# Seven products instead of eight for the third matrix of three feed-forwards, and second-matrix units spread between later pairs

## The reference

```python
# block 1, layers 0 and 1: feed-forwards 1 and 2
f = (jax.nn.silu(h @ ffn_w1[l]) * (h @ ffn_w3[l])) @ ffn_w2[l]
x = x + g2 * f
...
# block 2, layers 0 and 1: feed-forwards 3 and 4
gate, up = jnp.split(x @ w_ffn_in[i], 2, axis=-1)
ffn = (jax.nn.silu(gate) * up) @ w_ffn_out[i]
x = layer_norm(ALPHA * x + ffn + ple, ln2_g[i], ln2_b[i])
```

## Time and the profile before

| | us |
|---|---|
| median of 3 runs | 2541.24 |
| lowest and highest run | 2536.46, 2541.75 |
| profiled execution, its own time | 2539.25 |
| span of the profiled execution | 2537.5 |
| stretches of feed-forwards 2, 3, 4 | 361.7, 349.0, 349.0 |

### The profile page before, as it was taken

How to read it: one execution, slowest core, us unless ns; L and a number is a source line. 1 busy time by engine, 2 the same in 40 slices (tenths; PEclk the granted TensorE clock), 3 DMA queues, 4 the chain that set the end, 5 groups by cost and what they waited for, 6 DMA issues and landing times.

```text
span 2537.5 us, 32793 instructions
## 1 busy us (share of the span) xinstructions
PE 2453.0 (97%) x12859; PEld 2019.3 (80%) x12859; DVE 1584.6 (62%) x2380; ACT 1051.1 (41%) x1719; POOL 1038.1 (41%) x591
## 2 busy tenths in 40 slices
PE   7999999999999999999999999999999999999997
PEld 4777788888776787988677779898867777888896
DVE  5686877864487783644586476363568747645456
ACT  4335532333426542434443554343444355433342
POOL 0333453534325353435153355433514534553441
PEclk8999999999999999999999999999999999999998
DMA  8614335543222342332331213333323212333331
GB/s 283 200 50 133 117 133 183 189 159 102 86 82 94 122 131 89 103 94 99 102 84 58 67 65 102 100 96 104 100 81 83 75 50 67 99 101 100 100 100 50
DMA packets 239250, 268.73 MB, mean 106 GB/s; under 512 B 19592, under 2 KB 203640, under 8 KB 238840
## 3 DMA queue, kind: packets, MB, share of 16 engines
q1 hardware_dynamic: 239096, 266.63, 32.5%
HBM read 264.51 MB, written 2.10 MB: 105 GB/s over the span
## 4 chain that ended last, share of the span: by engine, by line
PE 79%; DVE 11%; ACT 3%; issue 3%; DMA 2%; POOL 1%; SPq 0%; ACTq 0%; DVEq 0%; POOLq 0%
PE bank L2730 24%; PE bank L2732 24%; PE bank L2731 24%; DVE r L1846 2%; DVE m_cv L2181 1%; DVE k_lo L1995 1%; POOL w_lo L1591 1%; DMA b_raw<-in_ada_w 1%; PE bank L3355 1%; ACT w_hi L992 1%; ACT k_hi L1046 1%; PE bank L3388 1%; DVE u_t_raw L2026 1%; DMA raw<-in_ffn_w 1%; PE bank L3050 1%
## 5 line engine op out<-in xcount | busy, mean ns | idle before, releaser
L1602 POOL TENSOR_TENSOR k_lo<-raw,k_hi 128x512 fp32r<-128x512 f32 x288 | 400.6, 1403 | 710.2 <-ACT k_hi L1046 707.3
L1046 ACT ACTIVATE k_hi<-raw 128x512 fp32r<-128x512 f32 x528 | 323.8, 627 | 471.2 <-PE bank L2732 371.8
L1591 POOL TENSOR_TENSOR w_lo<-raw,w_hi 128x2048 fp32r<-128x2048 f32 x53 | 248.1, 4681 | 534.1 <-ACT w_hi L992 452.7
L2730 PE MATMUL bank<-h_hi,k_lo 128*128 128x512 f32 (+1 forms) x1240 | 430.8, 347 | 3.8 <-DVE k_lo L1995 2.6
L2731 PE MATMUL bank<-h_lo,k_hi 128*128 128x512 f32 (+1 forms) x1240 | 429.4, 346 | 0.0
L2732 PE MATMUL bank<-h_hi,k_hi 128*128 128x512 f32 (+1 forms) x1240 | 429.1, 346 | 0.0
L2730 PE MATMUL bank<-h_hi,w_lo 128*128 128x512 f32 x800 | 323.0, 404 | 8.7 <-DVE h_lo L1955 3.9
L2732 PE MATMUL bank<-h_hi,w_hi 128*128 128x512 f32 x800 | 313.2, 391 | 0.0
L2731 PE MATMUL bank<-h_lo,w_hi 128*128 128x512 f32 x800 | 313.1, 391 | 0.0
L2730 PE MATMUL bank<-f_hi,k_lo 128*128 128x512 f32 x704 | 278.3, 395 | 10.3 <-DVE u_row L2054 8.3
L2731 PE MATMUL bank<-f_lo,k_hi 128*128 128x512 f32 x704 | 275.6, 391 | 0.0
(11 more groups left out here) (395 smaller groups left out, 4452.8 us busy)
## 6 DMA issues: line engine op xcount, KB each, us to landing
raw<-in_ffn_w SPq DMA_DIRECT2D x60, 1024.0 KB, 5.3
raw<-in_w_ffn_in SPq DMA_DIRECT2D x44, 1024.0 KB, 5.1
raw<-in_w_in SPq DMA_DIRECT2D x34, 1024.0 KB
b_raw<-in_ada_w SPq DMA_DIRECT2D x32, 1024.0 KB, 5.3
raw<-in_w_ffn_out SPq DMA_DIRECT2D x16, 1024.0 KB, 5.1
z_a<-in_ada_w SPq DMA_DIRECT2D x4, 2048.0 KB, 14.1
g_raw<-in_ada_w SPq DMA_DIRECT2D x8, 1024.0 KB, 5.8
raw<-in_w_out SPq DMA_DIRECT2D x8, 1024.0 KB
```

Of the source, the lines that this page charges most:

```text
L1046: act.activation(hi, src, ACT.Copy).then_inc(s.f_hi.up, 1)
L1591: pool.tensor_tensor(b.w_lo[p][:, 0:n], b.raw[p][:, 0:n], b.w_hi[p][:, 0:n].bitcast(F32), ALU.subtract)\
L1602: pool.tensor_tensor(lo, src, hi.bitcast(F32), ALU.subtract).then_inc(s.f_lo.up, 1)
L2730: pe.matmul(out, wlo, xhi, start=start, stop=False)
```

## The change

In feed-forwards 2, 3 and 4 a plan with `spread` is used. The third matrix's unit of pairs 4 to 10 (feed-forward 2) or 1 to 10 (3 and 4) becomes an *upper* unit: the same seven products as the first matrix's, with its own sums and additions, in banks 2, 6, 3, 7, and gating then multiplies two SBUF tiles. Passes have two pairs (the last three); from pair 3 on, two down units follow each pair, four remain for the end. Of a seven or upper unit DVE makes five low parts, of a down unit that of the second pair, POOL the others and all hidden low parts. Sums are made a fixed number of steps ahead (`summed`); feed-forwards 3 and 4 use two sets of sum buffers in turn. PE waits for each bank by itself, when the product that first writes it comes. In feed-forward 1 the units stay; low parts come ahead of sums at a step.

```diff
+SPREAD = [range(0, 2), range(2, 4), range(4, 6), range(6, 8), range(8, PAIRS)]
+SEVENS = "seven", "upper"
...
+    def __init__(self, early, spread, uppers=(), sets=(1,)):
+        self.units, self.spread, self.sets = [], spread, sets
+        self.passes = SPREAD if spread else PASSES
+        downs = [("down", n, j) for n in range(len(self.passes)) for j in range(KD // 2)]
+        upto = {pairs[-1] + AHEAD[n]: KD // 2 for n, pairs in enumerate(PASSES)}
+        if spread:
+            upto = {i: 2 for i in range(3, PAIRS)}
+        for i in range(PAIRS):
+            self.units += [("upper" if i in uppers else "plain", i, 0),
+                           ("whole" if early and i == 0 else "seven", i, 0)]
+            self.units += downs[:upto.get(i, 0)]
+            del downs[:upto.get(i, 0)]
+        self.units += downs
...
+        self.summed = {}
+        for u, (kind, _, _) in enumerate(self.units):
+            if kind in SEVENS and self.at[u, M6] >= RING:
+                t = next(t for t, qs in self.after.items() if self.at[u, M6] in qs)
+                self.summed[t - (3 if kind == "seven" and len(sets) > 1 else 1)] = u
...
     def on_vector(self, u, n):
         kind = self.units[u][0]
+        if self.spread and kind != "plain":
+            return u >= 2 and u < self.tail and (n == 1 if kind == "down" else n not in (M1, M7))
         return u >= 2 and (kind == "plain" or (kind == "seven" and n in (M2, M4, M3)))
...
         if kind == "seven":
-            return 0, 1, 4, 5
-        first = (6 if (i % 2 == 1) != (i >= len(PASSES[0])) else 2) if kind == "plain" else 2 * (u % 2)
+            return 0, 4, 1, 5
+        if kind == "upper":
+            return 2, 6, 3, 7
         if kind == "whole":
             first = 0
+        elif kind == "plain":
+            first = 6 if (i % 2 == 1) != (i >= len(PASSES[0]) and not self.spread) else 2
+        else:
+            first = 2 * (u % 2) if not self.spread or u >= self.tail else 6 if j % 2 else 2
...
-PLAN = {1: Plan(True), 2: Plan(False)}
+PLAN = [Plan(True, False), Plan(True, True, range(4, PAIRS))] + [Plan(False, True, range(1, PAIRS), (2, 1))] * DEPTH
...
-    if i:
-        old = max(v for v in range(u) if plan.units[v][0] == "seven")
+    if i >= len(plan.sets):
+        old = next(v for v, x in enumerate(plan.units) if x[0] in SEVENS and plan.nth(v) == i - len(plan.sets))
...
     def gated(i):
...
         for m in range(2):
             dve.wait_ge(*s.f_silu(n, 2 * i + (1 if m else 2)))
-            dve.tensor_tensor(b.f_full[:, m, :], b.f_act[:, m, :], bank[banks[m]][:, :], ALU.mult)\
+            other = b.f_full[:, m, :] if upper else bank[plan.banks(u)[m]][:, :]
+            dve.tensor_tensor(b.f_full[:, m, :], b.f_act[:, m, :], other, ALU.mult)\
                .then_inc(s.f_gated.up, 1)
...
-        if part == (M5 if kind == "seven" else 0) and u + 2 < plan.tail and plan.units[u + 2][0] == "seven":
-            dve_sums(dve, e, lay, u + 2)
+        if kind in SEVENS:
+            parts(u, kind, i, part)
         if kind == "down" and last:
             for m in range(2):
                 down(u, 2 * j + m, m)
         for q in plan.after[t - 1] if t else ():
             if plan.mine[q]:
                 dve_low_part(dve, e, lay, q)
+        if t in plan.summed:
+            dve_sums(dve, e, lay, plan.summed[t])
...
         for part in parts:
             at, v = AREA[part]
+            if part in (M1, M7, M5, M2):
+                bank_taken(u, at)
             pe.wait_ge(*s.low_in(n, plan, plan.at[u, part]))
```

More of the change, by code:

```diff
@@ L1077, in act_ffn @@
         kind, i, j = plan.units[u]
-        if kind == "seven" and part == M6:
-            first(u, i)
+        if kind in SEVENS and part == M6:
+            first(u)
         if kind == "seven" and part == M2:
@@ L1625, in pool_ffn @@
     for t, (u, part) in enumerate(plan.seq):
-        if part == 1 and plan.gate_done(u) is not None and plan.units[u][0] != "down":
+        if part == 1 and plan.gate_done(u) is not None and (plan.spread or plan.units[u][0] != "down"):
             hidden(plan.gate_done(u))
@@ L2030, in dve_ffn, with parts @@
     s, b, bank, plan, n = e.s, e.b, e.bank, lay.plan, lay.ffn
-    def parts(u, i, part):
+    def parts(u, kind, pair, part):
         first, second, third = b.u_row[:, LEFT_HALF], b.u_row[:, RIGHT_HALF], b.u_third[:, :]
+        areas, to = [bank[x] for x in plan.banks(u)], b.f_act if kind == "seven" else b.f_full
         def done(op):
             op.then_inc(s.f_part.up, 1)
-        i = plan.nth(i)
+        i = plan.nth(u)
         if part == M6:
             dve.wait_ge(*s.f_first(n, i + 1))
-            done(dve.tensor_tensor(second, first, bank[0][:, RIGHT_HALF], ALU.add))
+            done(dve.tensor_tensor(second, first, areas[0][:, RIGHT_HALF], ALU.add))
         if part == M7:
@@ L2046, in parts @@
             dve.wait_ge(*s.f_part(n, 5 * i + 1))
-            done(dve.tensor_tensor(third, second, bank[4][:, LEFT_HALF], ALU.add))
+            done(dve.tensor_tensor(third, second, areas[1][:, LEFT_HALF], ALU.add))
         if part == M4:
@@ L2057, in parts @@
             dve.wait_ge(*s.f_part(n, 5 * i + 4))
-            done(dve.tensor_tensor(b.f_act[:, 0, :], b.u_row[:, :], bank[5][:, :], ALU.add))
+            done(dve.tensor_tensor(to[:, 0, :], b.u_row[:, :], areas[3][:, :], ALU.add))
     def gated(i):
-        banks = next(plan.banks(u) for u, x in enumerate(plan.units) if x[:2] == ("plain", i))
-        if i:
+        u = plan.pair_units(i)[0]
+        upper = plan.units[u][0] == "upper"
+        if upper:
+            dve.wait_ge(*s.f_part(n, 5 * plan.nth(u) + 5))
+        elif i:
             dve.wait_ge(*s.fl(n, 2 * i))
@@ L2082, in dve_ffn @@
             gated(plan.gate_done(u))
-            if kind == "down":
+            if kind == "down" and not plan.spread:
                 hidden_low(plan.gate_done(u))
@@ L2418, in dve_shift_norm @@
     turn = 2 * DEPTH + 1 + l
-    ready = KD * (len(PASSES) - 1)
+    ready = KD * (len(lay.plan.passes) - 1)
     def take(k):
@@ L2905, in down @@
     def down(u, n_pass, j):
-        pairs = PASSES[n_pass]
+        pairs = plan.passes[n_pass]
         banks_free(u)
-        first = len(pairs) - (4 if u > plan.tail + 1 else 1)
+        first = 0 if u > plan.tail + 1 else len(pairs) - 1
         for k, i in enumerate(pairs):
@@ L2936, in pe_ffn @@
             pass
-        elif kind == "seven":
+        elif kind in SEVENS:
             if u == 1:
@@ L2940, in pe_ffn @@
                     pe.wait_ge(*lay.bank_free(m, USES[2]))
-            banks_free(u)
-            seven(u, i, range(7))
+            seven(u, range(7))
         elif kind == "plain":
@@ L3237, in fold @@
         row, off = bank[FOLD_AT[0]], FOLD_AT[1]
-        last = max(i for kind, i, _ in lay.plan.units[:u + 1] if kind == "seven")
+        last = max(v for v in range(u + 1) if lay.plan.units[v][0] == "seven")
         pe.wait_ge(*s.f_part(lay.ffn, 5 * lay.plan.nth(last) + 2))
```

161 lines of the change are left out of this document (83 added, 78 removed).

## The result

The changed kernel takes 2619.23 us, median of four runs (2617.35 to 2628.48), beside 2539.53 us for four runs of the kernel before: 1.0322 times as long, 95% interval 1.0294 to 1.0350. Forecast were 2548.7 us and a range of 2520 to 2575: the direction was right, the size and the range were not. The profiled execution is the longest of the four, 2628.48 us with a span of 2626.7; its mean granted clock is 0.970, that of the other three 0.972 to 0.974.

What follows compares the result with a forecast made beforehand. TensorE, busy 97% of the span, was taken as the bound. Cheaper matmuls -25.4, period stalls +25.2, feed-forward 2 +3.8 and tails +5.8 summed to +9.4 on 2539.25: 2548.7 us, range 2520 to 2575.

Steps and rivals of the forecast that it cites:

- The matmuls: Feed-forwards 2 to 4: 27 upper units take 9.96 us instead of 10.91, -25.4 us.
- DVE's load: Work added to DVE fits by its sum; DVE busy 270 to 290 us in feed-forward 3.
- the second rival: DVE is full, each POOL encounter costs 1.1, stall 3.3 a period: +37.6 us, 2576.9; chance 0.17.
- the large price: 1.1 us extra for a DVE instruction meeting POOL's, put on one of the next seven's sums.
- One period in 3 and 4: Feed-forwards 3 and 4: PE waits 1.8 us at M7 for bank 6, 14 times, +25.2 us.
- The step that failed: Feed-forwards 3 and 4: after each 1.8 us stall PE runs on, in step again a unit later.
- all stalls that I had counted: 25.2 us in periods of feed-forwards 3 and 4, 3.8 in feed-forward 2, 5.8 in the tails.
- The pairs before the first downs: Feed-forwards 3 and 4: only the second rival had DVE fall behind here, by 3.6 us more, +7.2.
- Feed-forward 2: First wait, at the first down's low part and then bank 6, 7.5 us instead of 3.7: +3.8 us.
- no stall in the steady periods: Feed-forward 2: the second down's evacuation, ready at about 19.6, meets PE's 20.8, so no wait.
- The tail: Feed-forwards 3 and 4: shorter last units uncover L3278's wait for DVE's norm sum, 2.9 us each, +5.8.
- Feed-forward 1 at nothing: Feed-forward 1: low parts reordered ahead of sums cost nothing, hidden behind the same matmuls.

Runs made afterwards that it cites:

- e12: Changed kernel with late sums, exchanged upper banks, other passes, feed-forward 1's old order, DVE's tail low parts and ACT's last silu first: 2514.7 us, 0.9901 of before.
- e11: e12 without the silu moved first and with plain units in place of the upper ones: 2534.4 us, 0.9974 of the kernel before.
- e2: Changed kernel with the next seven unit's sums made three steps later in feed-forwards 3 and 4: 2562.5 us, 1.0067 of the kernel before.
- e3: Changed kernel with plain units in place of the upper ones, spread passes and early sums kept: 2620.5 us, 1.0297 of the kernel before.
- e1: Changed kernel with TensorE running unneeded products during its waits for banks in feed-forwards 3 and 4: 2605.6 us, 1.0239 of the kernel before.
- e5: e2 with upper units using banks 6, 2, 7, 3 and down units' banks exchanged in feed-forwards 3 and 4: 2555.9 us, 1.0052 of before.
- e6: e2 with passes of pairs 0-2, 3-4, 5-6, 7-10 in feed-forwards 2, 3 and 4: 2551.8 us, 1.0034 of the kernel before.
- e8: e2 with all seven and upper units' sums in feed-forwards 2 to 4 at the last possible step: 2543.7 us, 1.0003 of the kernel before.
- e7: e2 with DVE's order of before, sums ahead of evacuations and low parts, in feed-forward 1: 2559.1 us, 1.0063 of the kernel before.

## Why the prediction was wrong

- **The matmuls, -25.4**: right in size (23.9 by PE's busy time in e12 against e11), the units 9.96 us as in the earlier trace rows.
- **DVE's load**: right, 280 us where 270 to 290 was forecast. It was not DVE's sum that cost: the second rival, in which DVE is full, fell with e2 and e3. In the period above two of the next seven's four sums took 1.75 and 1.77 us and two 0.68, where I had put one at the large price and one at 0.2 over the small; it is two large ones in all 14 periods.
- **One period in 3 and 4, 14 x 1.8 = 25.2**: the place, the mechanism and the count were right, and the 14 waits at M7 measured 34.0 (2.4 each): a term mis-sized by 9, for the second large sum, and in the two longest waits (3.6) for a block of 3.5 and 3.7 us before the load where the others have some 2.
- **The step that failed** is the sentence behind it: "PE stalls 1.8 us, then runs on and is in step again a unit later". It does not run on. Behind 7 of the 12 shorter waits in 3 and 4, and behind every longer one, it runs at 0.50 of the clock for 3.4 or 6.8 us. By the estimate above that made 32.2 us in all, nearly as much as all stalls that I had counted (25.2 + 3.8 + 5.8), and e1 showed it by itself. It is not the whole error: the stalls themselves came to 71.7 us, 36.9 more than counted, and the points before and behind this one say where. The trace of the kernel before held it: after the wait of 3.7 us in the earlier trace rows its windows read

```profile
952.60:956.30 3.70, 0.00 (x0) 0.00 (x0) 3.42 (x6) 1.48 (x3) 3.70 (x3) 1.00 0.33 107
956.50:959.90 3.40, 3.40 (x9) 2.66 (x10) 2.10 (x4) 2.58 (x6) 2.67 (x3) 0.50 0.50 175
```

- **The pairs before the first downs** were costed at nothing outside the second rival. Two waits of 7.1 us for the gating of pair 0 came there, which frees the first upper unit's bank (e2: sums ahead of it, then 2.9 left; e5: the bank). Two more, of 2.8 us, came at the first upper unit behind a down unit, where M1 wants a bank that a down unit filled; e6, in which these down units have three pairs and are longer, has neither.
- **Feed-forward 2, +3.8**: its first wait is 5.0 us where 7.5 was put, but not in the place that was costed. Neither the first down unit's low part nor bank 6 at M7 was waited for; the second down unit waited, for the bank that the plain unit of pair 3 holds until its gating:

```profile
970.98 0.77 PE L2764 MATMUL bank<-f_hi,k_lo 128*128 128x512 f32 x1 [4.97 <-DVE u_full L2100]
```

Before that gating DVE stood 3.5 us for the load at 962.96 (its sums). The nearness of 5.0 to 7.5 is luck. And "no stall in the steady periods" was wrong: 9.9 us for x, taken away by e8. The upper unit's sums, blocked for the load, stood in the same place.

- **The tail, 2 x 2.9**: right, 2.96 each (its clock again left out).
- **Feed-forward 1 at nothing**: wrong by 4 us in the profiled execution; the order of its sums is some 2 of them (e7). Hidden "behind the same matmuls" was not checked at the one wait for r, 1.5 us before, that was open already.

The range was made of PE's waits alone, so no case in it could pay for the clock.

## What to carry to other kernels

When an engine that does not set the time executes a hand-written list, look at what each instruction that can block (here sums that need a load) has behind it: in e3 a DVE busy half of the time delayed PE by 21 us in each of two feed-forwards, and moving four instructions three steps later took it away. Price a wait of TensorE by the wait and by what the granted clock does behind it, read from the nearest such wait in the trace of before. A saving on the busiest engine is only worth its sum once every wait that it uncovers is followed to its bank, its list and its queue; here the order of a few instructions and banks made the -25 us into +80, and with it mended the upper units bring some 20 (e12 against e11).

## What the runs showed of the hardware

- Waits of PE of 2.1 to 2.4 us, with PE busy on both sides of them, were followed by 3.4 us at the 1.2 GHz level in some cases and not in others (7 of 12 in the changed kernel). In e3 6 of the 14 gating waits in 3 and 4 (2.4 to 3.9 us) had it (10.2 and 17.1 us at half in 3 and 4, against 30.7 and 34.1); one of 3.1 us there had none, one of 2.1 us in the changed kernel had it. So the length of a wait alone does not decide it here; what does stays open.
- The same sum of two SBUF tiles took 0.68 or some 1.76 us within one group of four; the two long ones of the period above, at 1742.35 and 1744.16, run beside these low parts of POOL:

```profile
1740.17 3.41 POOL L1649 TENSOR_TENSOR f_lo<-u_full,f_hi 128x512 fp32r<-128x512 f32 x2 [1.29 <-ACT f_hi L1101]
1744.07 1.29 POOL L1629 TENSOR_TENSOR k_lo<-raw,k_hi 128x512 fp32r<-128x512 f32 x1 [0.49 <-ACT k_hi L1072]
```

  The Trainium skill ("SBUF — State Buffer", section Who interferes with whom) has it that a DVE instruction with two SBUF inputs contends with a GpSimd instruction that reads SBUF, under an exclusive lock. The rows agree; the 0.82 and 1.18 of the earlier trace rows show that an encounter need not cost a whole instruction of POOL.
